# Probabilities times V with V as the weights, two heads on two column groups

## The reference, cut

```python
def dsa_attend(q, ..., k, v, ...):                  # branch A, 8 query heads, 2 kv heads, head_dim 64
    logits = jnp.einsum('nqcgd,nqkcd->nqcgk', qg, ks) * HEAD_DIM ** -0.5 + bias
    probs = jax.nn.softmax(jnp.where(valid, logits, NEG), axis=-1)
    out = jnp.einsum('nqcgk,nqkcd->nqcgd', probs, vs)
...
def swa_attend(q, ..., k, v, ..., sinks, rel_bias): # branch B
    p = jnp.exp(logits - m[..., None])
    denom = p.sum(axis=-1) + jnp.exp(sink - m)
    o = jnp.einsum('...cgqk,...kcd->...qcgd', p, v) / denom
...
def layer_output(x, gate, p, att_a, att_b, w_oa, w_ob, w_out):
    o_a = (att_a * jax.nn.silu(p['a_z'])) @ w_oa
    o_b = (att_b * jax.nn.silu(p['b_z'])) @ w_ob
    merged = jax.nn.sigmoid(p['g_a']) * o_a + jax.nn.sigmoid(p['g_b']) * o_b
    return x + gate * (merged @ w_out)
```

## Time and profile before

| | |
|---|---|
| median of 3 runs | 1140.15 us (1138.95 to 1140.45) |
| span of the profiled execution | 1137.2 us |
| mean granted TensorE clock | 0.950 |
| PE busy | 1038.3 us (91%) |
| DVE, ACT, POOL busy | 677.6, 408.3, 322.8 us |
| DMA | 120.83 MB, mean 106 GB/s |

### The profile page before, as it was taken

How to read it: one execution, slowest core, us unless ns; L and a number is a source line. 1 busy time by engine, 2 the same in 40 slices (tenths; PEclk the granted TensorE clock), 3 DMA queues, 4 the chain that set the end, 5 groups by cost and what they waited for, 6 DMA issues and landing times.

```text
span 1137.2 us, 18078 instructions
## 1 busy us (share of the span) xinstructions
PE 1038.3 (91%) x6569; PEld 924.0 (81%) x6569; DVE 677.6 (60%) x1437; ACT 408.3 (36%) x1239; POOL 322.8 (28%) x348
## 2 busy tenths in 40 slices
PE   6976999999506999999999999999999999999998
PEld 1346887778306999999999898888888779999998
DVE  2666347899999999999600277645655464332111
ACT  0344556443102232212211467666655452222000
POOL 0043104111002443312213345322311023545442
PEclk9987999999857999999999889999999989999999
DMA  9731002222123322323213562211120536544332
GB/s 356 288 96 43 23 21 95 87 88 76 73 102 126 103 85 82 118 74 102 84 46 133 180 225 85 72 47 52 41 55 20 166 101 196 154 126 126 116 114 73
DMA packets 97490, 120.83 MB, mean 106 GB/s; under 512 B 11104, under 2 KB 79472, under 8 KB 96256
## 3 DMA queue, kind: packets, MB, share of 16 engines
q1 hardware_dynamic: 97408, 119.73, 32.9%
HBM read 89.72 MB, written 35.95 MB: 111 GB/s over the span
## 4 chain that ended last, share of the span: by engine, by line
PE 80%; DMA 8%; issue 4%; DVE 3%; ACT 3%; POOL 2%; POOLq 0%; SPq 0%; DVEq 0%; ACTq 0%
PE PS L1355 17%; PE PS L1357 17%; PE PS L1356 17%; PE PS L1608 9%; DMA snat<-STG 8%; PE PS L1584 6%; PE PS L1529 4%; PE PS L1364 4%; PE PS L1548 2%; PE PS L1587 2%; PE PS L1430 2%; DVE HL L1150 1%; DVE XT L1168 1%; POOL YO L879 1%; PE PS L1534 1%
## 5 line engine op out<-in xcount | busy, mean ns | idle before, releaser
L1355 PE MATMUL PS<-HH,WH 128*128 128x384 f32 (+1 forms) x576 | 189.2, 328 | 52.2 <-POOL WL L774 52.2
L1357 PE MATMUL PS<-HH,WL 128*128 128x384 f32 (+1 forms) x576 | 189.0, 328 | 0.0
L1356 PE MATMUL PS<-HL,WH 128*128 128x384 f32 (+1 forms) x576 | 188.9, 328 | 0.0
L774 POOL TENSOR_TENSOR WL<-RAW,WH 128x512 fp32r<-128x512 f32 (+1 forms) x80 | 100.4, 1260 | 300.2 <-ACT WH L895 300.1
L1209 DVE MAX8 M<-SC 128x8 f32<-128x384 f32 (+3 forms) x210 | 174.8, 870 | 10.5 <-DVE SC L1214 10.0
L1214 DVE MATCH_REPLACE8 SC<-M,SC 128x384 f32<-128x384 f32 (+3 forms) x210 | 179.9, 864 | 0.0
L1355 PEld LDWEIGHTS PS<-HH,WH 128*128 128x128 f32 x576 | 109.1, 189 | 52.7 <-POOL WL L774 52.7
L1355 PE MATMUL PS<-WH,HH 128*128 128x512 f32 (+3 forms) x288 | 110.3, 383 | 8.1 <-DVE HL L1150 7.9
L1356 PEld LDWEIGHTS PS<-HL,WH 128*128 128x128 f32 x576 | 109.0, 189 | 0.0
L1357 PEld LDWEIGHTS PS<-HH,WL 128*128 128x128 f32 x576 | 109.0, 189 | 0.0
L1356 PE MATMUL PS<-WL,HH 128*128 128x512 f32 (+3 forms) x288 | 108.7, 377 | 0.0
(11 more groups left out here) (180 smaller groups left out, 2068.1 us busy)
## 6 DMA issues: line engine op xcount, KB each, us to landing
RAW<-in_w_all SPq DMA_DIRECT2D x72, 256.0 KB, 2.7
WADA<-in_w_ada SPq DMA_DIRECT2D x8, 1536.0 KB, 20.1
gz<-STG SPq DMA_DIRECT2D x48, 192.0 KB, 1.8
snat<-STG SPq DMA_DIRECT2D x24, 256.0 KB, 2.0
QKV<-snat SPq DMA_DIRECT2D x8, 768.0 KB, 5.9
GT<-gz SPq DMA_DIRECT2D x32, 192.0 KB, 2.5
XN<-in_x_prompt SPq DMA_DIRECT2D x8, 512.0 KB, 16.8
btad<-bvd SPq DMA_DIRECT2D x4, 1024.0 KB
```

Source lines behind the costliest of these rows:

```text
L774: nc.gpsimd.tensor_tensor(WL[c % 2][:, k, 0:cw], RAW[:, n % 4, 0:cw], WH[c % 2][:, k, 0:cw].bitcast(F32), ALU.subtract).then_inc(lo_done, 1)
L1355: T.matmul(out, wh, mh, start=first, stop=False)
L1356: T.matmul(out, wh, ml, start=False, stop=False)
L1357: return T.matmul(out, wl, mh, start=False, stop=last)
```

## The change

Per pair of units (heads h and h+4, one of each kv head; the units are put in the order 0, 4, 1, 5, ...) and key block, V (128 x 64) is loaded as weights, once for each kv head, and P^T (128 x 128) streams. The first head's result goes to partitions 0 to 63 and the second's to 64 to 127 of the same columns of `bank(6 + br)`, so the group's result is feature-major and is not transposed; the rows of `w_o` and the columns of z are permuted on the host to fit. PV of both units is now issued at every second step. `PT` has three buffers in place of two. The division by the softmax sum now needs the reciprocals along the free axis, the same for 64 partitions: `RDEN` goes to DRAM transposed (`rdd`), comes back broadcast (`RB`), POOL multiplies it into z in place (in `ATS`), and DVE multiplies that with the bank.

```diff
+        HEADS = [4 * (i % 2) + i // 2 for i in range(8)]
+        UNITS = [(tt, br, h) for tt in range(NT) for br in range(2) for h in HEADS]
...
-        for g in range(2 * NT):
-            TP[8 * g + 15].append(("A", g // 2, g % 2))
...
-                if u >= 2:
-                    eng.wait_ge(pv_pe, u - 1)
+                if u >= 3:
+                    eng.wait_ge(pv_pe, (u - 3) // 2 + 1)
...
SP:
-                if s % 8 == 0 and 8 <= s < NU + 8:
+                if s % 8 == 1 and 9 <= s < NU + 8:
                     g = s // 8 - 1
+                    r = rows_of(g // 2)
+                    if g >= 2:
+                        sp.wait_ge(att_out[g % 2], 16 * (g // 2))
+                    sp.dma_start(ATS[:, g % 2, :, 0:r],
+                                 gz[512 * (g % 2):512 * (g % 2) + 512, tcols(g // 2)].rearrange("(b p) n -> p b n", p=128)).then_inc(zt_in, 16)
+                    sp.wait_ge(rden_done, g + 1)
+                    sp.dma_start(rdd[g, :, 0:r].rearrange("h q -> q h"), RDEN[0:r, g % 2, :], allow_slow_non_contiguous=True).then_inc(rdd_out, 16)
+                if s % 8 == 2 and 10 <= s < NU + 8:
+                    g = s // 8 - 1
+                    r = rows_of(g // 2)
+                    sp.wait_ge(rdd_out, 16 * (g + 1))
                     if g >= 1:
-                        wait_evac(sp, TIDX[("A", (g - 1) // 2, (g - 1) % 2)])
-                    sp.dma_start(ZT[:, :, 0:rows_of(g // 2)],
-                                 gz[512 * (g % 2):512 * (g % 2) + 512, tcols(g // 2)].rearrange("(b p) n -> p b n", p=128)).then_inc(zt_in, 16)
+                        sp.wait_ge(zr_done, g)
+                    for kv in range(2):
+                        sp.dma_start(RB[HD * kv:HD * (kv + 1), :, 0:r],
+                                     bass.AP(rdd.tensor, 1024 * g + 512 * kv, [[0, HD], [128, 4], [1, r]])).then_inc(rb_in, 16)
...
-                for x in TP.get(s - 1, []):
-                    if x[0] == "A":
+                if s % 8 == 6 and 14 <= s < NU + 8:
+                    g = s // 8 - 1
+                    sp.wait_ge(att_done, g + 1)
...
POOL:
+                if s % 8 == 3 and 11 <= s < NU + 8:
+                    g = s // 8 - 1
+                    r = rows_of(g // 2)
+                    pool.wait_ge(zt_in, 16 * (g + 1))
+                    pool.wait_ge(rb_in, 32 * (g + 1))
+                    z = ATS[:, g % 2, :, 0:r]
+                    nc.gpsimd.tensor_tensor(z, z, RB[:, :, 0:r], ALU.mult).then_inc(zr_done, 1)
...
DVE:
-                if (s - 11) % 8 == 0 and 11 <= s <= NU + 3:
-                    g = (s - 11) // 8
+                if s % 8 == 1 and 9 <= s <= NU + 1:
+                    g = s // 8 - 1
...
+                    V.reciprocal(RDEN[0:r, br, :], DEN[0:r, br, :]).then_inc(rden_done, 1)
+                if s % 8 == 4 and 12 <= s <= NU + 4:
+                    g = s // 8 - 1
+                    r = rows_of(g // 2)
+                    dve.wait_ge(pv_pe, 4 * (g + 1))
+                    dve.wait_ge(zr_done, g + 1)
+                    z = ATS[:, g % 2, :, 0:r]
+                    V.tensor_tensor(z, bank(6 + g % 2).rearrange("p (b n) -> p b n", b=4)[:, :, 0:r], z, ALU.mult).then_inc(att_done, 1)
...
PE:
-                if 0 <= s - 3 < NU:
-                    u = s - 3
+                if 0 <= s - 3 < NU and s % 2 == 0:
+                    u = s - 4
...
                     for b in range(kb):
                         m = min(128, nk - 128 * b)
+                        for kv in range(2):
+                            half = slice(HD * kv, HD * (kv + 1))
...
+                            last = T.matmul(PS[half, 6 + br, 128 * h:128 * h + r], v, PT[(u + kv) % 3][0:m, 128 * b:128 * b + r],
+                                            start=(b == 0), stop=(b == kb - 1))
```

More of the change, by code:

```diff
@@ L146, in build_program @@
         SD = small("SD", [128, 8])
-        RDEN = small("RDEN", [128, 8])
+        RDEN = small("RDEN", [128, 2, 8])
         IN2 = [at(f"IN{i}", [128, 6, 2, HD], F32R, off[0] + 3072 * i) for i in range(2)]
@@ L175, in build_program @@
         VBS = at("VBS", [128, 2, 128], F32, 132608)
[L176 to L179, removed]
+        XNB = at("XNB", [128, 20, HD], F32, XB + 8192)
+        XG = at("XG", [128, 20, HD], F32, XB + 13312)
+        LG = [at("LG0", [128, 1024], F32, XB), at("LG1", [128, 1024], F32, XB + 4096)]
         PB = [at("PB0", [128, 1024], F32, SCB), at("PB1", [128, 1024], F32, SCB + 4096), at("PB2", [128, 1024], F32, off[0] + 4096)]
-        ZT = at("ZT", [128, 4, 128], F32, XB + 21504)
-        PT = at("PT", [128, 2, 1024], F32, SCB + 8192)
+        RB = at("RB", [128, 4, 128], F32, 67584)
+        PT = [at("PT0", [128, 1024], F32, SCB + 8192), at("PT1", [128, 1024], F32, SCB + 12288),
+              at("PT2", [128, 1024], F32, XB + 18432)]
         KSC = at("KSC", [128, 2, 4, HD], F32R, SCB + 16384)
@@ L292, in build_program @@
         sink_act = sem("sink_act")
+        rden_done = sem("rden_done")
+        rdd_out = sem("rdd_out")
+        rb_in = sem("rb_in")
+        zr_done = sem("zr_done")
         att_done = sem("att_done")
@@ L372, in build_program @@
         SHEADS = [(tt, h) for tt in SCORED for h in range(4)]
-        UNITS = [(tt, br, h) for tt in range(NT) for br in range(2) for h in range(8)]
+        HEADS = [4 * (i % 2) + i // 2 for i in range(8)]
+        UNITS = [(tt, br, h) for tt in range(NT) for br in range(2) for h in HEADS]
         NU = len(UNITS)
@@ L421, in build_program @@
         for q, (_, x) in enumerate(TQ):
-            if x[0] == "A":
-                EV.append("V")
-            elif x[0] == "P" and unit_keys(x[1]) > 512:
+            if x[0] == "P" and unit_keys(x[1]) > 512:
                 EV.append("SV"[x[2]])
@@ L471, in t_evac @@
                 last = copy(QT[x[1] % 2][:, 4 * x[2]:4 * x[2] + 4, 0:r], src[:, :, 0:r])
[L472 to L477, removed]
             else:
@@ L1072, in _ @@
             act.wait_ge(min_done, NU)
-            act.wait_ge(pv_pe, NU)
+            act.wait_ge(pv_pe, NU // 2)
             for half in range(2):
@@ L1314, in _ @@
                         link(V.tensor_tensor(DEN[0:r, 1, :], DEN[0:r, 1, :], ES[0:r, 0, :], ALU.add))
-                    link(V.reciprocal(RDEN[0:r, :], DEN[0:r, br, :]))
-                    dve.wait_ge(pv_pe, 8 * (g + 1))
                     if g >= 2:
[L1318 to L1321, removed]
+                        dve.wait_ge(rdd_out, 16 * (g - 1))
+                    V.reciprocal(RDEN[0:r, br, :], DEN[0:r, br, :]).then_inc(rden_done, 1)
[6 more added lines that the diff above has]
+                    V.tensor_tensor(z, bank(6 + g % 2).rearrange("p (b n) -> p b n", b=4)[:, :, 0:r], z, ALU.mult).then_inc(att_done, 1)
             for q in range(2, 4):
@@ L1529, in transposes @@
                         last = T.transpose(out[0:m, 128 * (b % 4):128 * (b % 4) + r], PB[u % 3][0:r, 128 * b:128 * b + m], IDF[0:r, 0:r])
[L1530 to L1534, removed]
                 else:
@@ L1600, in _ @@
                     kb = (nk + 127) // 128
-                    kv = slice(HD * (h // 4), HD * (h // 4) + HD)
                     for b in range(kb):
                         m = min(128, nk - 128 * b)
[L1604 to L1609, removed]
+                        for kv in range(2):
+                            half = slice(HD * kv, HD * (kv + 1))
+                            if br == 0:
+                                v = VAS[0:m, b, half] if tt == SAMPLE else VA[0:m, b, half] if tt else VA0[:, half]
+                            else:
+                                v = VBS[0:m, b, half] if tt == SAMPLE else VB[0:m, max(tt - 1, 0) + b, half]
+                            last = T.matmul(PS[half, 6 + br, 128 * h:128 * h + r], v, PT[(u + kv) % 3][0:m, 128 * b:128 * b + r],
+                                            start=(b == 0), stop=(b == kb - 1))
                     last.then_inc(pv_pe, 1)
@@ L1659 @@
     spans = ((1280, 1604), (0, 768), (1604, 2372), (768, 1280), (2372, 2884), (2884, 4932))
+    pair = np.arange(512).reshape(2, 4, HD).transpose(1, 0, 2).reshape(-1)
+    w_all = np.concatenate([w_in[:, a:b] for a, b in spans], axis=1)
+    zc = IDX_W + NAT_W
+    w_all[:, zc:zc + D] = w_all[:, zc + np.concatenate([pair, 512 + pair])]
     def cols(v):
@@ L1672 @@
         "x_prompt": x["x_prompt"][0], "x_sample": x["x_sample"][0],
-        "w_all": np.concatenate([w_in[:, a:b] for a, b in spans], axis=1),
-        "w_ada": x["w_ada"][0], "w_o": np.concatenate([x["w_oa"][0], x["w_ob"][0]], axis=0), "w_out": x["w_out"][0],
+        "w_all": w_all,
+        "w_ada": x["w_ada"][0], "w_o": np.concatenate([x["w_oa"][0][pair], x["w_ob"][0][pair]], axis=0), "w_out": x["w_out"][0],
         "cache_ak": x["cache_a_k"].reshape(PAST, 128), "cache_av": x["cache_a_v"].reshape(PAST, 128),
```

20 lines of the change are left out of this document (9 added, 11 removed).

## The result

| | us |
|---|---|
| changed kernel, median of 4 runs | 1330.61 (1328.24 to 1331.22) |
| kernel before, median of 4 runs beside them | 1139.67 (1138.95 to 1140.45) |
| ratio, 95% interval | 1.1672 [1.1656, 1.1689] |
| forecast | 1156 (1120 to 1190) |

The change makes the kernel 191 us slower.

What follows compares the result with a forecast made beforehand. PE was taken to set the pace, running only two units ahead of DVE. Terms of -25, -12.5, +44 and +9 us gave +15.5 on the median of 1140.15: 1156 us, range 1120 to 1190.

Steps and rivals of the forecast that it cites:

- PV and dropped transposes: Attention on PE: new PV matmuls net -25 us after handovers, attention transposes gone -12.5 us.
- order on SP's queue: RB's loads stand behind big transfers: 12 us lost in tile 0, 7 us in the prompt's last B group.
- B groups' 12: Branch B's groups: the new product waits behind the next tile's split on POOL; losses 4.4, 4.2, 2.3, 1.0, 0.
- D1: Transposed store of a group's reciprocals to DRAM, 1024 pieces of 4 bytes: taken as 2.5 us, ends 1.3 and 3.0.
- Rival 4: D1 is slow, 5 us, because of 4-byte pieces: 1181 us in all; chance 0.12.
- Rival 1: In PV the two column groups don't stream together, so the 41 us gain goes: 1189 us; chance 0.14.
- Handovers: Array width changes on entering and leaving PV cost 0.14 us each, 64 pairs x 2: 18 us.
- Rival 2: Handovers around PV cost nothing, 18 us less: 1138 us; chance 0.17.
- rival 3: Small transfers pass big ones on the queue, so tile 0 and group 15 behave like the others: 1135 us; chance 0.12.
- The chain's stalls and the clock: Waits for the reciprocals' way through DRAM and POOL to DVE, +44 us, and slow clock restarts, +9 us.
- The clock: PE stops of some 4 us in the attention stage cost slow restarts: +9 us, bounds 0 and 20.
- The end: First output matmul waits for WOL(0), queued behind the last product on POOL: 5 us later.

Runs made afterwards that it cites:

- experiment 2: Changed kernel without the reciprocals' store, their broadcast loads and GpSimd's product, so the division is missing: 1109.92 us, ratio 0.9742 to the kernel before.
- experiment 1: Changed kernel with a group's reciprocals stored as 128 pieces of 32 bytes in place of 1024 of 4 bytes: 1184.59 us, ratio 1.0394 to the kernel before.
- 5: As experiment 1, with BTA's load issued one step later and the early loads behind RB instead of ahead: 1168.52 us, ratio 1.0257 to the kernel before.
- experiment 6: As 5, with GpSimd's product put ahead of the norm and the split: 1150.12 us, ratio 1.0085 to the kernel before.
- experiment 8: Changed kernel storing 128 pieces per group, size and pitch varied, one execution: 4-byte pieces took 6.80 us at pitch 4, 1.42 at 32.
- experiment 3: As experiment 2, with the two heads of a pair one after the other, each with all its blocks: 1134.54 us, ratio 0.9956 to the kernel before.
- experiment 4: As experiment 3, with V loaded at its full width of 128 columns for either head: 1159.03 us, ratio 1.0174 to the kernel before.

## Why the forecast was right in sign and wrong in size

The runs split the 191 us, with the names of the forecast's terms:

| term | forecast | measured | from |
|---|---|---|---|
| PV and dropped transposes | -37.5 | -29.8 | experiment 2 less before |
| order on SP's queue (tile 0, last B group) | +19 and their restarts | +16.1 | 1 less 5 |
| GpSimd's queue | in the B groups' 12 | +18.4 | 5 less 6 |
| rest of the chain, with the clock that it costs | the rest of 53 | +40.2 | 6 less 2 |
| D1 above the 1.4 us of 32-byte pieces | in the terms above, as 2.5 | +146.0 | changed kernel less 1 |

**The failed step is the size of D1**, "D1 has no row; a store of 8 KB landed in 1.3 us and one of 64 KB in 3.0. I take these as the ends for both, and 2.5 for D1". With 1024 pieces of 4 bytes side by side it is 9.1 to 10.4 us in 14 of the prompt's 16 groups and 8.0 and 8.9 in the sample tile. In the other two, where SP issues big transfers between the store and RB, the loads come 13.7 and 16.5 us after the store; of the 16.5, SP's own issue of ORAW takes 14.78. The bounds came from stores of large pieces; by bytes this one is smaller than either, and by its pattern it has no neighbour among the rows. Rival 4 named the right step at half its size, and its reason, pieces of 4 bytes, is only half the cause: in experiment 8 such pieces land in 1.4 us when they are 32 bytes apart.

From store to loads the changed kernel takes 146 us longer than experiment 1 over the 18 groups, and the time is 146 us longer. That the two agree so well is in part luck. DVE's stalls are only 124 us longer (197.1 against 72.7), since in the B groups GpSimd's split hides part of D1: in group 2 (an A group) the stall grows by 7.9 us of 8.1, in group 3 by 6.1 of 7.9. PE's idle time is 118 us longer, and its busy time 26 us, because the stops lower the clock.

By the runs, stores of 128 pieces of 8, 16 and 32 bytes take 1.4 us at a pitch of 32, and 4-byte pieces just as long; of the 128-piece stores, only those with several pieces in one stretch of 32 bytes took longer by their form. The Trainium skill ("DMA: Bandwidth & Descriptors", Specifications) says that below 512 bytes a transfer does a read-modify-write. No run here shows whether something is read; the row of 32-byte pieces at 1.4 us shows that falling below that size is not enough to be slow.

**The other points.**
- *PV side by side*: right. 0.055 us per record, 0.058 forecast; experiment 3 shows that the overlap makes it. Rival 1 is out.
- *Handovers*: right within what the starts show. On entering, 0.094 us over the normal start and 0.05 on the second pair (not all of it the handover's, experiment 4); on leaving 0.202 where 0.084 was before, 0.12 more. Rival 2 is out.
- *The sum of the PE terms*: 8 us too good. PE idles 5 us more in the stage of experiment 2, waiting for DVE and ACT; this was nowhere in the sum.
- *Transfers pass in order*: right in its effect, rival 3 is out. In group 15 the issue of ORAW blocks SP as well.
- *The chain's stalls and the clock*: too small even apart from D1. Experiment 1 has a D1 1.1 us shorter than forecast and still costs 75 us over experiment 2, not under 53. DVE's stalls are 72.7 us in it: 3.0 to 6.0 in each B group of the prompt before the last. With a lead of 1.4 that leaves 1.6 or more each time; the forecast let PE's loss fall from 4.4 to nothing by the fifth.
- *The clock*: 9 us were forecast with an upper bound of 20. PE's busy time, over the same matmuls, is 1049.9 us in the changed kernel, 1023.5 in experiment 1 and 1003.8 in experiment 2. Each record's busy time multiplied by the clock granted to it gives 969, 973 and 976 us, the same work within 1%. So slower clocks stretch PE's own work by some 46 and 20 us. The window at 1010 to 1120, where stops are longest, is granted 0.58.
- *The end*: first output matmul (1119.91) 16.0 us after the last PV (1103.95), 4.3 before. It waits for WOL, as forecast; of the 7 us over the forecast's 9.1, D1 has 5.6 and the loads 1.5.

```profile
1104.43 0.60 SPq L684 DMA_DIRECT2D rdd<-RDEN  x1
1112.48 1.24 SPq L692 DMA_DIRECT2D RB<-rdd  x2
1116.83 0.72 POOL L859 TENSOR_TENSOR ATS<-ATS,RB 128x256 f32<-128x256 f32 x1 [18.22 <-DMA RB<-rdd]
1117.51 6.18 POOL L870 TENSOR_TENSOR WOL<-ORAW,WOH 128x1024 fp32r<-128x1024 f32 x2
...
1119.91 0.69 PE L1372 MATMUL PS<-ZH,WOH 128*128 128x384 f32 x1 [15.07 <-POOL WOL L870]
```

**Still open**: why the chain in its best order varies so between executions. The one that was traced, the slowest, is 50.8 us longer than experiment 2's, 26.5 of it idle PE and 24.3 slower matmuls; how the 40 us of the medians divide, no trace shows. Open too is what makes side-by-side pieces slow in the memory: the runs show by which distances, not by what, nor whether it matters that neighbours come from different rows of `RDEN`.

## What to carry to other kernels

When a new wait stands in a loop that has only two steps of lead, count on paying nearly its whole latency. Here 146 us more between store and loads cost 118 us of idle PE and 26 us of slower matmuls. Price a small transposing store by where its pieces fall, not by its bytes or by a store of large pieces: if no row has its pattern, the upper bound is open, and the range must say so. A few values per row can be broadcast on PE, by a matmul of the repeated column with the identity, for 0.93 us a group; the way through DRAM took 6.5 to 7.0 us from the reciprocal to DVE's product in most groups of the best order tried (experiment 6) and 14.8 in a typical one of the changed kernel.

## What the runs showed of the hardware

- A store of 128 pieces of 4 bytes to DRAM lands in 1.4 us when they are 32 bytes or more apart, in 6.8 (7.0 in another run) when they are side by side, though its packets end 1.03 us after the issue in both.
- 1024 pieces instead of 128, each with its own 64 bytes, cost 2 us more (3.47).
- Half-width fp32 matmuls of 128 columns on the two column groups start in pairs 0.006 to 0.007 us apart, one pair each 0.109 us; on one group alone, one each 0.109; at full width, one each 0.112.
- From the last start of PV to the first of QK it is 0.031 us when PV is at full width, 0.202 when it is at half width (128 streamed columns in both).
- Issuing two loads of 0.5 MB right behind 3 MB took SP 14.78 us, in which it issued nothing else.
